# A fused two-block fp32 transformer kernel: the input x in four transfers, matmuls ahead of the first unit, and the last mixer's attention steps moved apart

## The reference

```python
h = rms_norm(x, norm_mix[0]);  qkv = h @ w_qkv            # the start
...
z = h @ w_mix_in[l]                                        # the last mixer
q, k, v, xr, yr = jnp.split(z, split_pts, axis=-1)
def block(qblk):                                           # 4 heads, blocks of 128 queries
    s = jnp.einsum('bqhmd,bkhmd->bhmqk', qblk, k)          # two score maps (m = 0, 1)
    p = jax.nn.softmax(s, axis=-1)
    w = p[:, :, 0] - lam * p[:, :, 1]
    return jnp.einsum('bhqk,bkhe->bqhe', w, v)
o = rms_norm_2(o, subln_g) * (1.0 - lambda_init)           # per head
rec = recurrent_group(xr, yr, ...)                         # conv, gated scan, gelu
return jnp.concatenate([attn, rec], axis=-1) @ w_mix_out[l]
```

## Time and profile before

| | |
|---|---|
| median of 3 runs | 2382.03 us |
| the profiled execution | 2382.01 us, span 2380.2 us (1.8 us lie around the span) |
| TensorE matmul busy | 2336.3 us, 98% of the span |
| VectorE, ScalarE busy | 1440.3 us (61%), 1038.3 us (44%) |
| TensorE's granted clock, mean | 1.000 |
| chain that ended last | TensorE 91%, VectorE 5%, ScalarE 3%, issue 1% |

### The profile page before, as it was taken

One profiled execution on the slowest core, in us unless ns is written; L12 is line 12 of the kernel. 1 busy time (PEld: TensorE's weight loads), 2 busy tenths in 40 slices (PEclk: granted clock), 3 DMA queues, 4 the chain that ended last, 5 costly groups with the idle time before them and its releaser, 6 DMA issues.

```text
span 2380.2 us, 30886 instructions
## 1 busy us (share of the span) xinstructions
PE 2336.3 (98%) x11342; PEld 1981.6 (83%) x11342; DVE 1440.3 (61%) x2073; ACT 1038.3 (44%) x1562; POOL 0.2 (0%) x4
## 2 busy tenths in 40 slices
PE   7999999999999999999999999999999999999999
PEld 5788888888888886888888888888877677888887
DVE  7877777767566677867566575333356986433333
ACT  5655555544233347854223333323346565322333
POOL 0000000000000000000000000000000000000000
PEclk9999999999999999999999999999999999999999
DMA  4222222235444531024444533332322112323231
GB/s 156 80 80 80 79 79 77 77 103 177 140 161 159 174 117 64 1 72 168 159 150 159 177 102 108 105 100 95 115 71 67 58 54 71 97 94 110 93 111 54
DMA packets 71246, 249.57 MB, mean 105 GB/s; under 512 B 9824, under 2 KB 10336, under 8 KB 70752
## 3 DMA queue, kind: packets, MB, share of 16 engines
q1 hardware_dynamic: 68912, 247.28, 31.1%
q10 hardware_dynamic: 2224, 0.79, 0.1%
HBM read 245.94 MB, written 2.10 MB: 104 GB/s over the span
## 4 chain that ended last, share of the span: by engine, by line
PE 91%; DVE 5%; ACT 3%; issue 1%; DMA 0%; SPq 0%; ACTq 0%; DVEq 0%
PE psum L432 27%; PE psum L434 27%; PE psum L433 27%; PE psum L496 2%; PE psum L885 1%; PE psum L527 1%; PE psum L556 1%; PE psum L549 1%; PE psum L939 1%; DVE w_lo L1734 1%; PE psum L989 1%; DVE x L2249 0%; PE psum L969 0%; PE psum L532 0%; DVE y L2247 0%
## 5 line engine op out<-in xcount | busy, mean ns | idle before, releaser
L432 PE MATMUL psum<-h_hi,w_hi 128*128 128x512 f32 x1768 | 681.6, 386 | 7.6 <-DVE w_lo L1734 2.7
L433 PE MATMUL psum<-h_lo,w_hi 128*128 128x512 f32 x1768 | 670.1, 379 | 0.0
L434 PE MATMUL psum<-h_hi,w_lo 128*128 128x512 f32 x1768 | 670.1, 379 | 0.0
L1069 ACT ACTIVATE w_hi<-raw 128x1024 fp32r<-128x1024 f32 x385 | 403.2, 1052 | 454.8 <-PE psum L434 445.0
L1734 DVE TENSOR_TENSOR w_lo<-raw,w_hi 128x1024 fp32r<-128x1024 f32 x385 | 466.0, 1220 | 133.3 <-ACT w_hi L1069 131.9
L432 PEld LDWEIGHTS psum<-h_hi,w_hi 128*128 128x128 f32 x1768 | 334.2, 189 | 62.5 <-issue 9.3
L433 PEld LDWEIGHTS psum<-h_lo,w_hi 128*128 128x128 f32 x1768 | 334.3, 189 | 47.6 <-issue 2.6
L434 PEld LDWEIGHTS psum<-h_hi,w_lo 128*128 128x128 f32 x1768 | 334.2, 189 | 47.4
L2227 DVE TENSOR_TENSOR s_s<-s_g,psum 128x512 f32<-128x512 f32 x44 | 30.3, 688 | 275.6 <-issue 224.2
L432 PE MATMUL psum<-f_hi,w_hi 128*128 128x512 f32 x512 | 194.0, 379 | 0.0
L433 PE MATMUL psum<-f_lo,w_hi 128*128 128x512 f32 x512 | 194.0, 379 | 0.0
(11 more groups left out here) (343 smaller groups left out, 3252.8 us busy)
## 6 DMA issues: line engine op xcount, KB each, us to landing
raw<-stream SPq DMA_DIRECT2D x385, 512.0 KB, 3.5
ada_raw<-ada_in SPq DMA_DIRECT2D x72, 512.0 KB, 4.0
x<-x_in SPq DMA_DIRECT2D x2, 1024.0 KB, 6.4
out<-x SPq DMA_DIRECT2D x8, 256.0 KB, 2.4
a_mask<-mask_in SPq DMA_DIRECT2D x1, 1024.0 KB, 9.4
crow<-crow_in SPq DMA_DIRECT2D x2, 512.0 KB, 4.5
gatew<-gate_in ACTq DMA_DIRECT2D x2, 256.0 KB, 3.7
a_cos<-rope_in SPq DMA_DIRECT2D x1, 256.0 KB, 7.8
```

The lines of the kernel that those rows point to most:

```text
L432: nc.tensor.matmul(o, whi, xh, start=start, stop=False)
L433: nc.tensor.matmul(o, whi, xl, start=False, stop=False)
L434: return nc.tensor.matmul(o, wlo, xh, start=False, stop=stop)
L1069: A(w_hi[:, slot(u0), :], raw[:, slot(u0), :], ACT.Copy).then_inc(S["hi"], 1)
```

## The change

- x arrives in four transfers of 512 KB (`x_in0` to `x_in3`), one ahead of `cols` and the first unit, three behind it. ScalarE makes two tiles of `a_oh`, not four, before it splits unit 0, and VectorE likewise; all eight squares come after the split of unit 1.
- VectorE sets a 128x128 piece of `rst` to 1 at the very start, and TensorE makes 20 matmuls of 128 columns on it before unit 0. Nothing reads their result.
- In the last mixer, place m now holds the scores of block m, the transposes of block m-2 and the value products of block m-3, with a place 18 at step 159, the last. `m_w` has two buffers, so that the weights of block m wait for the transposes of block m-2.
- `c_output` of heads 0 to 2 moves from places 5, 9, 13 to places 6, 10, 14; `c_sum` of heads 1 and 2 moves from the steps of places 10 and 14 to two steps behind them; `c_sum` of head 3 moves from step 156 to behind the loop, ahead of `outward`; `c_output(3)` stands behind `m_rec_high(2)`, and `c_norm(3)` behind the loop on ScalarE.

```diff
-SOFT_AT = [9 * MIX + 39 * i // 8 for i in range(18)]
+SOFT_AT = [9 * MIX + 39 * i // 8 for i in range(19)]
-SUM_AT = (SOFT_AT[7], SOFT_AT[10], SOFT_AT[14], 19 * MIX + 4)
+SUM_AT = (SOFT_AT[7], SOFT_AT[10] + 2, SOFT_AT[14] + 2)
...
-        m_w = at("m_w", [P, T], arena + 77 * KB)
+        m_w = (at("m_w0", [P, T], arena + 77 * KB), at("m_w1", [P, T], arena + 90 * KB))
...
-            sp.dma_start(x[:, 0:4, :], x_in[:, 0:4, :]).then_inc(S["x_in0"], 16)
+            def load_x(p):
+                sp.dma_start(x[:, 2 * p:2 * p + 2, :], x_in[:, 2 * p:2 * p + 2, :]).then_inc(S[f"x_in{p}"], 16)
+
+            load_x(0)
             sp.dma_start(cols[:], cols_in).then_inc(S["col_in"], 16)
             load_unit(0, 0)
-            sp.dma_start(x[:, 4:8, :], x_in[:, 4:8, :]).then_inc(S["x_in1"], 16)
+            for p in range(1, 4):
+                load_x(p)
             load_unit(1, 1)
...
+            pe.wait_ge(*after("wz", 0))
+            for _ in range(20):
+                nc.tensor.matmul(bank(6, P), rst[:, 1, 0:P], rst[:, 1, 0:P], start=True, stop=True)
             unit(0, 0, bank(0), a_oh, a_ol, lambda k: after("E_lo", k))
...
                         if m < 16:
                             c_scores(m)
-                        if 1 <= m < 17:
-                            c_turn(m - 1)
-                        if m >= 2:
-                            c_values(m - 2)
+                        if 2 <= m < 18:
+                            c_turn(m - 2)
+                        if m >= 3:
+                            c_values(m - 3)
...
                 last.then_inc(S["mm"], 1)
+
+            c_sum(3)
...
-            for k in range(4):
+            for k in range(2):
                 first_high(k)
             split(0)
-            for k in range(2):
-                first_square(k)
-            for k in range(4, KT):
+            for k in range(2, KT):
                 first_high(k)
             split(1)
-            for k in range(2, KT):
+            for k in range(KT):
                 first_square(k)
...
-                        if 1 <= m < 17:
-                            c_copy(m - 1)
+                        if 2 <= m < 18:
+                            c_copy(m - 2)
                         if m < 16:
                             c_exps(m)
-                        if m >= 5 and m % 4 == 1:
+                        if m >= 6 and m % 4 == 2 and m < 18:
                             c_output(m // 4 - 1)
...
                 if n == 19:
-                    c_norm(3)
-                    act.preload_act_table_set("exp_and_others")
                     m_rec_high(2)
+                    c_output(3)
                 m_evac(n)
                 if n >= 16:
                     m_gelu_square(n - 16)
+            c_norm(3)
+            act.preload_act_table_set("exp_and_others")
             c_high(3)
...
-                if m:
-                    dve.wait_ge(*after("C_T", m - 1))
-                V.tensor_scalar(m_w[:], m_p[:, 0, :], rden[:, 0:1], None, ALU.mult).then_inc(S["C_w"], 1)
+                if m >= 2:
+                    dve.wait_ge(*after("C_T", m - 2))
+                w = m_w[m % 2]
+                V.tensor_scalar(w[:], m_p[:, 0, :], rden[:, 0:1], None, ALU.mult).then_inc(S["C_w"], 1)
...
-            c_norm(3)
             m_rec_low(2)
             m_gelu_cube(3)
+            c_norm(3)
```

More of the change, by code:

```diff
@@ L239, in build @@
         S = {}
-        names = ("col_in E_hi E_lo gz mm lo hi raw0 raw1 raw2 raw3 x_in0 x_in1 par_in tab_in msk_in pre_a pre_v pre_p btab gw_in cpos_in out_st "
+        names = ("col_in E_hi E_lo gz mm lo hi raw0 raw1 raw2 raw3 x_in0 x_in1 x_in2 x_in3 wz par_in tab_in msk_in pre_a pre_v pre_p btab gw_in cpos_in out_st "
                  "A_evac A_sq A_sh A_sl A_ms A_ln A_rst A_qn A_rt A_rope A_vt A_V A_S A_pad A_mx A_exp A_p A_T A_pt "
@@ L977, in c_turn @@
                     pe.wait_ge(*after("C_pt", m - 1))
-                transposes(m_w[:], bank(4), RES).then_inc(S["C_T"], 1)
+                transposes(m_w[m % 2][:], bank(4), RES).then_inc(S["C_T"], 1)
             def c_values(m):
@@ L1256, in first_high @@
             def first_high(k):
-                act.wait_ge(S[f"x_in{k // 4}"], 16)
+                act.wait_ge(S[f"x_in{k // 2}"], 16)
                 A(stored(a_oh[:, k, :]), by_parity(x[:, k, :]), ACT.Copy, scale=col("norm_mix", k)).then_inc(S["E_hi"], 1)
             def first_square(k):
-                collected_squares("N", 0, k, x[:, k, :], (S[f"x_in{k // 4}"], 16))
+                collected_squares("N", 0, k, x[:, k, :], (S[f"x_in{k // 2}"], 16))
             def first_split(j):
@@ L1765, in first_norm_low @@
                 V.tensor_tensor(h_lo[:, k, :], nrm[:, k % 2, :], f32(h_hi[:, k, :]), ALU.subtract).then_inc(S["N_lo"], 1)
+            V.memset(rst[:, 1, 0:P], 1.0).then_inc(S["wz"], 1)
             dve.wait_ge(S["col_in"], 16)
-            for k in range(4):
+            for k in range(2):
                 first_low(k)
             low(0, 0)
-            collect("N", 0, 1)
-            for k in range(4, KT):
+            for k in range(2, KT):
                 first_low(k)
             low(1, 1)
-            for k in range(2, 7):
+            for k in range(1, 7):
                 collect("N", 0, k)
@@ L2350, in c_weights @@
                 V.tensor_scalar(rden[:, 1:2], rden[:, 1:2], small[:, 56:57], None, ALU.mult).then_inc(S["C_rd"], 1)
-                if m:
-                    dve.wait_ge(*after("C_T", m - 1))
-                V.tensor_scalar(m_w[:], m_p[:, 0, :], rden[:, 0:1], None, ALU.mult).then_inc(S["C_w"], 1)
+                if m >= 2:
+                    dve.wait_ge(*after("C_T", m - 2))
+                w = m_w[m % 2]
+                V.tensor_scalar(w[:], m_p[:, 0, :], rden[:, 0:1], None, ALU.mult).then_inc(S["C_w"], 1)
                 dve.wait_ge(*after("C_w", 2 * m))
                 dve.wait_ge(*after("C_rd", 2 * m + 1))
-                V.scalar_tensor_tensor(out=m_w[:], in0=m_p[:, 1, :], scalar=rden[:, 1:2], in1=m_w[:],
+                V.scalar_tensor_tensor(out=w[:], in0=m_p[:, 1, :], scalar=rden[:, 1:2], in1=w[:],
                                        op0=ALU.mult, op1=ALU.add).then_inc(S["C_w"], 1)
```

## The result

| | before, same sessions | changed |
|---|---|---|
| median | 2381.88 us (2381.20 to 2382.18, 12 runs) | **2387.51 us** (2386.26 to 2389.83, 12 runs) |
| ratio | | 1.0026, 95% interval 1.0018 to 1.0033 |
| profiled execution, span | 2382.01, 2380.2 us | 2387.41, 2385.6 us |

The changed kernel is **slower, by 5.6 us**. The forecast was 2381.9 and its range ended at 2385.5.

What follows compares the result with a forecast made beforehand. TensorE's matmuls are busy 98% of the span, so only its idle and slow time can be won. Terms -5.2 - 1.3 + 2.8 + 3.6 = -0.1 us on 2382.01 gave 2381.9 us, 8-in-10 range 2378.0 to 2385.5.

Steps and rivals of the forecast that it cites:

- the fall of the clock: Rival at the mixer loop's end: the stall drops the clock, 13 slow matmuls, 2.8 us more, 2384.7 us; chance 0.14.
- -5.2 for the start: Start: earlier transfers win 2.5 us and the lifted clock 2.8, with 0.1 us charged, so 5.2 us won.
- +5.1 for the mixer: Last mixer: 1.3 us won on waits, 2.8 and 3.6 us lost at the sums of squares.
- The first term: Start: with 512 KB less in front, x and unit 0's weights land earlier and TensorE begins at 8.55, 2.5 us won.
- x does not arrive sooner: Rival at the start: transfers served side by side, the start loses 1.3 of its 5.2 us, 2383.2 us; chance 0.07.
- The second term: Start: 20 small matmuls lift the clock before unit 0, whose first 13 matmuls then run at full clock, 2.8 us won.
- The rival that they wouldn't: Start: the small matmuls don't lift the clock, the start wins 1.5 us instead of 5.2, 2385.6 us; chance 0.08.
- VectorE's products at 0.68 us each stay ahead of TensorE: Step at the start: VectorE's products keep ahead of unit 0 on TensorE, which needs 0.65 us for a tile.
- Won: 1.3 us: Mixer: the transposes' 2.4 us of waits for `m_w` go, part returns at `c_scores`, 1.3 us won.
- The sums, 2.8 and 3.6 us: Mixer: TensorE waits 1.4 us twice for squares of heads 1 and 2, and 3.6 us for head 3's.
- The rival that the sums don't wait: Mixer: squares are ready in time, losses of 6.4 us vanish, 2375.5, or 2376 to 2379 us; chance 0.13.
- The argument against it: Against a clock fall in the stall: TensorE's longest idle time after the start was 2.17 us, with the clock still 2.4 GHz.

Runs made afterwards that it cites:

- e3: e1 with x brought in two halves instead of four pieces; 2380.10 us, ratio 0.9991 against the kernel before.
- e4: The changed kernel with the start of the kernel before, so the mixer change alone; 2389.79 us, ratio 1.0033 against the kernel before.
- e9: The changed kernel with sums of heads 1 and 2 two steps later and head 3's behind the output units' second tile; 2380.46 us, ratio 0.9995.
- e5: e1 with nine unused small matmuls in TensorE's gap at 50 to 52 us; 2378.99 us, ratio 0.9989 against the kernel before.
- e12: e1 with TensorE held ahead of unit 0 until all eight products of x are made; 2384.23 us, ratio 1.0009 against the kernel before.
- e1: The kernel before with only the start of the change, the mixer left as before; 2379.16 us, ratio 0.9990.
- e2: e1 without the 20 small matmuls on the ones; 2379.85 us, ratio 0.9992 against the kernel before.
- e7: The changed kernel with the sums of heads 1 and 2 two steps later; 2384.47 us, ratio 1.0013 against the kernel before.
- e6: The changed kernel with 14 unused small matmuls in the stall at the loop's end; 2386.15 us, ratio 1.0019 against the kernel before.
- e8: The changed kernel with the sum of head 3 behind the second tile of the output units; 2383.28 us, ratio 1.0007 against the kernel before.

## Why the prediction was wrong

**The sign of each part was right. Two terms of the start were far too large, the mixer's gain was not there, and the fall of the clock, set aside as a rival, happened.** The forecast was -5.2 for the start and +5.1 for the mixer; measured were -2.7 and +7.9.

*The first term, "2.5 us won" by the transfers, failed.* I had x's first part at 4.5 and the weights at 6.1, by taking 1.3 us per 512 KB off the rows of before. They landed at 5.2 and 8.1. With x in halves the weights came at 7.4 to 7.6 (before, e3, e4). In the ten profiles with four pieces they came six times between 6.7 and 7.2, once at 7.5 (e9) and three times between 7.9 and 8.2 (the changed kernel, e5, e12), so the forecast 6.1 is never reached; e1 has 6.9, which is why its start stands 0.9 us ahead of the changed kernel's. What failed is the rule that 512 KB less in front make a landing 1.3 us earlier. The 1.3 us came from later rows; in the first 4 us only 0.46 MB had moved in the changed kernel and 0.61 in the one before. And not all that moves is in front: when the changed kernel's weights landed, 1.9 MB had moved, and only 1.16 MB of it was x's first part, `cols` and the weights. The rival "x does not arrive sooner" comes nearer, but is not what happened: its first part was to land with the second, and they landed at 5.2 and 9.3 us.

*The second term, "2.8 us won" by the clock, failed in what follows, not in the clock.* The small matmuls did lift the clock: at 8.01 us in the changed kernel, where it rose at 16.62 before, and in the others with this start between 4.97 and 8.01. The rival that they wouldn't is false. They started at 1.80, not at 1, and ended at 9.5, not at 8.1. The step that failed is "VectorE's products at 0.68 us each stay ahead of TensorE": beside unit 0 at the full clock the rows of ScalarE's products grow from 0.75 to 1.00 us and VectorE's to 0.88 (e1, e2, e12). TensorE needs 0.65 us for a tile, and they came every 0.83 (the changed kernel) to 0.87 us (e1). So ScalarE and VectorE set the pace at the end of unit 0 and kept unit 1's `w_lo` back. The price of 2.8 us was itself that of one execution: 13 matmuls were slow before, 14 in e4, nine in e2. Without the lift e2 lost 2.0 us; 1.1 of them went to the slower products and 0.3 behind them, and the lift is worth 0.6 to 0.7 us (e1 against e2). By both terms the sums of squares stood at 21.94 and not at 18.9.

*"Won: 1.3 us" in the mixer came to nothing, though its mechanism was right.* The wait came back at `c_scores` as forecast: 0.81 us at place 2 (0.9 forecast) and 0.31 at place 3, beside the 0.75 at place 1 that before had as 0.77. That is 1.1 of the 2.4 us, the very number of the forecast. What it put at nothing are 0.3 us more at `m_tmp` and TensorE's own rows: by the waits 1.0 us is won, and in e9 TensorE's rows between these marks are 0.8 us longer in sum. Its 156.03 us, less the 1.0 us that sums and `rst` still wait, are the 155.03 of before, so that nothing is left.

*The sums, 2.8 and 3.6 us, were right*: 1.3, 1.5 and 3.5 us, for the reasons given. The repairs show it: by the marks 1.8 and 4.8 us came back when they were moved, by the medians 3.0 and 4.2 (that of head 3 with the clock's 1.5 in it, less a wait of 0.28 that is left). The rival that the sums don't wait is false.

*The clock in the stall was chosen wrong.* I had the case as a rival at 0.14, at 2.8 us and 2384.7 us. It happened, in the profiles of the changed kernel, of e4 and of e7, and e6 shows what it costs: 1.5 us in the profile and 1.4 in the medians. The price was too high because at the start the low clock lasted 13 matmuls, and here it lasted 3.4 us. The argument against it, that the clock had stayed up behind a gap of 2.17 us, was drawn from one execution. In the profiles of e3, e7 and e8 the clock fell behind that very gap.
The Trainium skill, "TensorE: Matmul & The Clock Gate", section "Why this matters for your kernels", warns of an idle gap between bursts of matmuls, and I gave it too little weight; the trace agrees with it in the stall of 3.5 us, and has falls behind idle times of 2.17 us as well.

So the mixer's 7.7 us by the marks are 5.3 of waits (5.1 forecast), 1.5 of the clock (0.5 ahead of outward and 1.1 behind it, e6 against the changed kernel) and 0.9, mostly of longer rows, which weren't forecast. Together: 2381.9, plus 2.5 for the start, 0.2 for the waits, 1.5 for the clock and 0.9 for the rows gives 2387.0; measured were 2387.5. Why the rows are longer stays open. My range was too narrow because the failing terms all had the same sign, and I had set their bounds one by one.

## What to carry to other kernels

Move a consumer earlier only as far as its producer's chain allows: three sums moved by a few steps cost 6.3 us of waiting, and of the 2.4 us of waits that the move was to remove 1.4 came back at other instructions. In a kernel whose TensorE is 98% busy a stall costs its length and perhaps another 1.5 us of slow clock behind it, as some of 2.2 us and all of 3.5 us did here; in e6 useless small matmuls in the gap prevented it. And a warmed-up TensorE is only worth what its feeders can keep up with: cost their work from rows taken beside a fast TensorE, not beside a slow one.

## What was not expected of the hardware

- Twenty fp32 matmuls of 128 columns, begun at 1.80 us, raise the granted clock from 1.2 to 2.4 GHz 3.2 to 6.2 us later, as the work of before did 5.5 us, that of e4 6.0 and that of e2 3.9 us after its first matmul.
- Behind the idle time of 2.17 us at about 50 us the clock fell in three of the twelve profiles that have it unfilled (e3, e7, e8), and stayed up in the others, those of before, the changed kernel and e1 among them; in e12 it fell behind two waits of 0.78 and 1.44 us. In the stall of 3.5 us it fell in each of the three profiles that have it unfilled (the changed kernel, e4, e7). Each of these low stretches lasted 3.4 us; those behind 2.17 us cost 1.4 to 1.8 us, that in the stall 1.5.
- ScalarE's product of 128x512 took 0.744 us with TensorE idle, 0.752 with TensorE at 1.2 GHz and 1.003 with TensorE at 2.4 GHz reading the tiles that are being written; VectorE's 0.744, 0.747 and 0.884. ScalarE's split and its squares beside the same matmuls were not longer in e1 (1.06 against e12's 1.05 us, 1.13 against 1.14 for two) and at most 0.12 us longer in any profile.
- The landing of 512 KB issued at the same time in the same program start varied from 6.7 to 8.2 us over the profiles of the kernels with four pieces of x, without a difference in what was queued ahead of it.
